# One line's shift of x in SBUF, and pieces out of order in three projections

## The reference

```python
def first_block(x, ...):
    y = _retention_layer(x, a_w_in[0], a_w_out[0])          # 4 heads, width 2048
    x = _layer_norm(DEEPNORM_ALPHA * x + y, ln_g[0], ln_b[0])
    shared = _shared_latent_kv(x, kv_w_down, kv_norm, kv_w_up)
    y = _mla_layer(x, b_w_in[0], ..., b_w_out[0], *shared)  # 16 heads, width 2048
    x = _layer_norm(DEEPNORM_ALPHA * x + y, ln_g[1], ln_b[1])
    return x
def second_block(x, ...):
    h = rmsnorm(x, norm_mix_g[0])
    proj = h @ w_in[0]
    ...                                                     # pooling and neighbourhood attention
    x = x + jnp.concatenate([a, b], axis=-1) @ w_out[0]
    h = rmsnorm(x, norm_mlp_g[0])
    x = x + jnp.square(jax.nn.relu(h @ w_up[0])) @ w_down[0]
    return rmsnorm(x, final_g)
```

## Time and profile before

| what | value |
|---|---|
| median of the runs shown | 1385.91 us |
| span of the profiled execution | 1385.1 us |
| PE busy | 1367.3 us, 99% |
| DVE, ACT, POOL busy | 73%, 54%, 22% |
| matmuls | 7308 |
| granted PE clock | 0.999 of full speed |
| HBM traffic | 248 GB/s over the span |

### The profile page before, as it was taken

The page is one execution under the profiler, slowest core; times in us unless marked ns, Lnnn a source line. Parts: engine busy times, 40 slices in busy tenths (PEclk is TensorE's granted clock), DMA queues, the critical chain, the costliest instruction groups (busy, mean ns, idle before and its releaser), DMA issues.

```text
span 1385.1 us, 19133 instructions
## 1 busy us (share of the span) xinstructions
PE 1367.3 (99%) x7308; PEld 1182.2 (85%) x7308; DVE 1008.2 (73%) x1671; ACT 745.7 (54%) x1197; POOL 305.8 (22%) x161
## 2 busy tenths in 40 slices
PE   8999999999999999999999999999999999999998
PEld 7788888888888888888888888778888999998887
DVE  7979687889933755554555479936868887889895
ACT  5453535466544443344334446648956556576554
POOL 2050414110134444333433310025213000000000
PEclk9999999999999999999999999999999999999999
DMA  7458575475367988965796556354122675455552
GB/s 268 165 177 232 196 203 174 141 280 203 135 191 216 320 206 236 279 185 150 227 280 183 164 213 260 140 191 127 53 85 76 176 210 151 144 180 213 191 192 103
DMA packets 53898, 260.37 MB, mean 188 GB/s; under 512 B 5568, under 2 KB 10304, under 8 KB 28224
## 3 DMA queue, kind: packets, MB, share of 16 engines
q1 hardware_dynamic: 37152, 163.04, 33.6%
q0 software_dynamic: 5760, 41.95, 15.4%
q10 hardware_dynamic: 10912, 54.40, 10.9%
HBM read 252.03 MB, written 91.23 MB: 248 GB/s over the span
## 4 chain that ended last, share of the span: by engine, by line
PE 80%; DVE 13%; DMA 3%; ACT 2%; issue 1%; SPq 0%; POOL 0%; DVEq 0%; ACTq 0%; POOLq 0%
PE bank L614 21%; PE bank L616 21%; PE bank L615 21%; PE bank L1336 6%; PE bank L1398 3%; PE bank L1287 3%; DVE wlo L2291 3%; PE bank L1315 1%; DVE wlo_a L2291 1%; DMA v_spill<-v_tok 1%; DMA cols<-in_cols 1%; DMA stage<-in_w 1%; DMA stage<-tsum 1%; DVE ar_lo L2291 1%; DVE xres L2469 1%
## 5 line engine op out<-in xcount | busy, mean ns | idle before, releaser
L793 POOL TENSOR_TENSOR wlo<-stage,whi 128x1024 fp32r<-128x1024 f32 (+2 forms) x68 | 169.1, 2512 | 436.6 <-ACT whi L1618 350.3
L1621 ACT ACTIVATE whi<-stage 128x1024 fp32r<-128x1024 f32 (+2 forms) x155 | 148.2, 1002 | 111.1 <-PE bank L616 92.3
L2291 DVE TENSOR_TENSOR wlo<-stage,whi 128x1024 fp32r<-128x1024 f32 (+1 forms) x133 | 152.8, 1177 | 13.9 <-ACT whi L1621 13.8
L614 PE MATMUL bank<-xhi,whi 128*128 128x256 f32 (+1 forms) x300 | 98.6, 329 | 1.6 <-POOL wlo L929 1.2
L616 PE MATMUL bank<-xhi,wlo 128*128 128x256 f32 (+1 forms) x300 | 98.5, 328 | 0.0
L615 PE MATMUL bank<-xlo,whi 128*128 128x256 f32 (+1 forms) x300 | 98.5, 328 | 0.0
L1618 ACT ACTIVATE whi<-stage 128x1024 fp32r<-128x1024 f32 (+2 forms) x74 | 76.1, 1079 | 19.7 <-issue 14.6
L2291 DVE TENSOR_TENSOR wlo_a<-stage,whi_a 128x1024 fp32r<-128x1024 f32 (+1 forms) x60 | 71.6, 1217 | 15.2 <-ACT whi_a L1621 15.2
L614 PE MATMUL bank<-whi,xhi 128*128 128x512 f32 (+1 forms) x204 | 78.3, 384 | 2.1 <-DVE wlo L2291 1.2
L616 PE MATMUL bank<-whi,xlo 128*128 128x512 f32 (+1 forms) x204 | 77.3, 379 | 0.0
L615 PE MATMUL bank<-wlo,xhi 128*128 128x512 f32 (+1 forms) x204 | 77.2, 378 | 0.0
(11 more groups left out here) (499 smaller groups left out, 4332.8 us busy)
## 6 DMA issues: line engine op xcount, KB each, us to landing
stage<-in_w SPq DMA_DIRECT2D x71, 1024.0 KB, 5.0
tsum<-in_w ACTq DMA_DIRECT2D x32, 1024.0 KB, 12.2
stage<-tsum SPq DMA_DIRECT2D x32, 1024.0 KB, 4.8
tsum<-in_w POOLq DMA_DIRECT2D x16, 1024.0 KB, 10.0
tsum<-tsum POOLq DMA_DIRECT2D x16, 1024.0 KB, 9.9
stage<-in_w SPq DMA_DIRECT2D x8, 1152.0 KB, 6.9
usum<-in_w POOLq DMA_DIRECT2D x8, 1024.0 KB, 10.0
stage<-usum SPq DMA_DIRECT2D x32, 256.0 KB, 3.9
```

Source lines behind the costliest of these rows:

```text
L614: pe.matmul(dst, a_hi, b_hi, start=start, stop=False, skip_group_check=onto)
L793: pool.tensor_tensor(lo[:, r], stage[p % 2][:, r], hi[:, r].bitcast(F32), ALU.subtract).then_inc(w_lo, 1)
L1621: act.activation(dst, src, ACT.Copy, scale=scale).then_inc(signal, 1)
L2291: dve.tensor_tensor(dst, src, hi.bitcast(F32), ALU.subtract).then_inc(signal, 1)
```

## The change

First, the five small buffers are placed ahead of `s_hi2` and x, not behind `ident`. Everything from `s_hi2` to `ident` moves up by 448 bytes, 7 lines: `s_hi2`, `s_lo2`, `xhi`, `xlo`, `vs_b` (and `comb`, `stage2`, `xres`, `grow`, `ident`, which are no matmul weights) begin at line 1 modulo 8. `oT` and all behind it stay at their bytes, and so do the weight buffers before it. Second, in `seven`, a 512-column product reads its moving operand and writes its PSUM bank in pieces out of order: both get the same rearranged access pattern, so the result is the same.

```diff
@@ after gap("gap_a", 256)
+        cols = sb("cols", [P, COLS])
+        stat = sb("stat", [P, TT, 2, 6])
+        mv = sb("mv", [P, TT, 2])
+        small = sb("small", [P, 4, 8])
+        eps = sb("eps", [P, 4])
         with ExitStack() as h:
             s_hi2 = sb("s_hi2", [P, PK, HALF], F32R, h)
@@ after ident = sb("ident", [P, P])
-        cols = sb("cols", [P, COLS])
-        stat = sb("stat", [P, TT, 2, 6])
-        mv = sb("mv", [P, TT, 2])
-        small = sb("small", [P, 4, 8])
-        eps = sb("eps", [P, 4])
@@ after ADD, SUB = ALU.add, ALU.subtract
+        WALK = {AO.w: (2, 2), BO.w: (2, 4), DN.w: (4, 2)}
+
+        def walked(x, a, b):
+
+            return x.rearrange("p (a b n) -> p b a n", a=a, b=b)
@@ in seven
-                        last = split_dots(pe, to, s_hi[:, kk, r], s_lo[:, kk, r], wh[:, kk, c0:c1], wl[:, kk, c0:c1],
+                        b_hi, b_lo = wh[:, kk, c0:c1], wl[:, kk, c0:c1]
+                        if c1 - c0 == 512:
+                            to, b_hi, b_lo = (walked(x, *WALK[st.w]) for x in (to, b_hi, b_lo))
+                        last = split_dots(pe, to, s_hi[:, kk, r], s_lo[:, kk, r], b_hi, b_lo,
```

## The result

The changed kernel takes 1389.16 us, the median of 18 runs (1387.7 to 1393.1), beside 1386.18 us for the kernel before on the same chip (18 runs, 1384.81 to 1386.99). The ratio is 1.0025, with a 95% interval of 1.0018 to 1.0031: slower by about 3 us. The prediction was 1372.0 us and faster by over 0.2% at 0.72. The time lies inside the range, but the direction is wrong, and the two terms of the sum that carried the gain are what has to be explained.

What follows compares the result with a forecast made beforehand. PE's matmuls were taken to bound the kernel, each with a fixed 13.3 ns excess. Span 1385.1 - 8.9 (pieces) - 6.0 (x or `vs_b` stationary) + 1.0 (returned) = 1371.2 us; with 0.8 to the median, 1372.0; range 1359 to 1393.

Steps and rivals of the forecast that it cites:

- What bounds the kernel: Whole kernel: PE busy 99% of the span at full clock, waits 11.4 us, so what a matmul costs is the kernel's cost.
- Small buffers: `cols`, `stat` and `eps` are moved, not resized, with every reader and writer in place: nothing.
- What comes back: PE's waits on other engines, such as loads and weight splits, return part of the gain: 1.0 us.
- the reading of rows 7: Six 256-column neighbourhood-attention products, stationary one line behind, moving in two pieces: 113.3 ns each, excess 6.7 instead of 13.3.
- Pieces in the seven-block projections: 1332 walked matmuls, 408 with `s_hi2` stationary, each gain 6.7 ns: -8.9 us, upper bound +12.1.
- x or `vs_b` stationary, one line behind: 900 matmuls with the stationary operand at line 1, moving weights at 2, gain 6.7 ns each: -6.0 us, upper bound +8.2.
- x moving, one line behind the stationary weights: 1776 matmuls with the distance of the other sign: taken as nothing, bounds -11.8 and +23.6 us.
- x trails and pays for it: Rival: in `gate_product`, `feature`, `turned_product` and up-projection, moving x runs into the stationary load: 1387.2 to 1394.6 us, chance 0.12.
- Only the address pays: Rival: the walk gives nothing at equal lines, 1308 matmuls gain 8.7 us by address: 1377.8 us, chance 0.08.
- Pieces cost in PSUM: Rival: writing output in pieces costs 9.1 ns for each of 1332 matmuls, 12.1 us: 1392.0 us, chance 0.06.
- a walked product on `dr` staying at 226.7: Test: three 512-column products in pieces should take 220 ns each; staying at 226.7 would make the prediction wrong.

Runs made afterwards that it cites:

- E1: Address half of the change alone, no pieces in the seven-block projections, against the kernel before: 1389.01 us, ratio 1.0022.
- E3: Kernel without the three layers, 48 matmuls for each of 40 settings of distance, width and walk, executed once: 226.7 to 233.3 ns at 512 columns.
- E6: Matmuls alone, more widths and 64, 32 or repeated stationary columns; with 32, 231.7 ns (512 columns) and 113.3 (256) at distances 0, 1 and 3.
- E2: Pieces alone, every buffer where it was in the kernel before: 1385.73 us, ratio 0.9999.
- E8: Kernel before with x 12 lines further on, distance 4 to the weights, nothing else: 1385.66 us, ratio 0.9998.
- E10: Matmuls alone, 22 after an entry matmul of 300 to 312 columns, ten distances; distance 3 with 256 columns: 113.3 or 117.8 ns by entry.
- E9: Kernel before with small buffers moved, x 12 lines later, all up-projection weights and c one line further in: 1377.43 us, ratio 0.9937.
- E12: E9 unchanged, run again, against the kernel before: 1380.73 us, ratio 0.9953.

## Why the prediction was wrong

*What bounds the kernel* held: the waits went from 11.9 to 10.6 us, DVE's busy time moved by 3 us, and what a matmul costs is what the kernel costs. *Small buffers* was rightly nothing. *What comes back* was put at 1.0 us for a gain over the whole kernel; the runs show about that much, 1.1 us, for the 256-column products alone, as a wait for `eight` that the kernel before did not have (0.2 us in E1).

**The step that failed first is the reading of rows 7.** "The excess is a fixed price for each matmul, whatever its columns" was read from rows 4 to 6, and rows 7 were taken for a relief from that price that would travel to other widths. The excess is a result of width, load and distance together (E3, E6)., which the prediction called as a witness that another distance changes nothing, could not show it: four lines apart are the same as none, and 320 columns take 146.7 ns at every distance that was measured. Rows 7 showed distance 1 at 256 columns, and not a settled pace of it. The settled pace is 117.8 ns, with and without the pieces (E3), a relief of 2.2 ns where the prediction took 6.7. The 96 products of this kind stand in groups of six among products of 512 columns, and their mean is 115.5 ns in the kernel before and 117.1 in the changed one; there six of the same products at the same addresses take 978.12 - 977.42 = 0.70 us, 116.7 each, where the earlier trace rows had 0.68:

```profile
977.42 0.28 PE L620 MATMUL bank<-npt_hi,nv_hi 128*128 128x256 f32 x1
...
978.12 0.28 PE L1473 MATMUL bank<-nz 128*128 128x256 f32 x1
```

*Pieces in the seven-block projections*, -8.9 us: nothing (E2: ratio 0.9999; E3: every walk at the pace of its straight twin). Rows 7 differed from rows 5 in two things, the prediction said that no row separates them, and then gave the term to both. The 408 of them with `s_hi2` stationary pay 2.2 ns for their distance, +0.9 us.

*x or `vs_b` stationary, one line behind*, -6.0 us: distance 1 at 512 columns costs 2.2 ns a matmul, +1.8 us in the account, and nothing for the 84 with 320 columns. The other end, +8.2, had the right sign.

*x moving, one line behind the stationary weights*, nothing between -11.8 and +23.6: two effects of opposite sign, +5.2 us at 512 columns and -4.5 at 256. One price for both widths was the error. The sum, +0.7, is close to the nothing that was taken, and that is luck: each effect alone is over six times as large. Of the 18.3 us between the forecast of the pace (-14.9) and the account (+3.4), the two terms before have 9.8 and 7.8. The rival *x trails and pays for it* came nearest, with 1387.2 us at its mild end. It had the right place and sign for 512 columns, but at its upper end twice the price (13.3 against 6.7), and without the gain at 256. *Only the address pays* was right about the pieces (modulo 8, and as E8 shows modulo 4, they read the same lines) and wrong about what the address pays. *Pieces cost in PSUM* fell with E2: the Trainium skill's rule (page "PSUM — Partial Sum Buffer", section "Specifications (TRN2)") that a non-contiguous access pattern slows matmuls significantly does not hold for pieces of 64 and 128 columns here, which cost less than a measurement can tell.

The Trainium skill's rule of two independent SBUF read ports (page "TensorE: Matmul & The Clock Gate", section "Step-by-step: what each phase is for") would have given 1385.9 us, nearer than the forecast, but its reason does not hold here. The trace disagrees: distance alone moved the pace between 226.7 and 233.3 ns (E3), and with 32 stationary columns it moved nothing (E6). That load and moving stream meet somewhere is inferred from this; no run shows where.

Of the tests that the prediction set, a walked product on `dr` staying at 226.7 and x moving off by more than 2 ns both came out against it.

Left open: by what mechanism the distance of a load and a stream in SBUF, modulo four lines, comes to set the pace, and why the sign depends on the width. The map gives the paces; no run here looks inside.

## What to carry to other kernels

When PE sets the pace and its matmuls differ only in operands, read the distance between starts per class of width and of relative start address, and measure a class before pricing it; a map of 40 settings, 381 us of device time, would have spared the wrong extrapolation from six matmuls. Never carry a per-matmul saving from one width to another. If two things differ between the row that shows the gain and the row that does not, separate them first, and check that the row shows a settled pace: six matmuls cannot. Before splitting the difference of two spans into causes, read the granted clock of both over short stretches: 3.4 us at half the clock were worth 2 us here, more than half of what was to be explained.

## What had not been expected of the hardware

- With 128 stationary columns the pace depends on the distance of the moving and the stationary operand's start addresses modulo four 64-byte lines: 226.7 to 233.3 ns at 512 columns, 113.3 to 120.0 at 256. At 224, 192 and 128 columns it is 111.7 ns at every distance that was measured (E3, E6).
- The same instructions at the same addresses have two stable paces, 113.3 and 117.8 ns; a shift of the entry by 1.7 ns selects one (E10). The ten executions of one whole kernel fall in two groups of time, 3 to 4 us apart (E9, E12); that the two paces make them is likely and not shown.
- These steady paces fit one grid of 6.67 ns, 16 cycles of 2.4 GHz: 113.3, 120.0, 226.7 and 233.3 are 17, 18, 34 and 35 of them, and 117.8 and 228.9 are 53 and 103 of them over three matmuls. Other paces, 111.7 or 231.7 for instance, come out only over four matmuls or more, where a fit says little. After a stall some matmuls pass before a stretch is on it.
